# A whole model block on one core: first panel's low halves on VectorE, head 0 loaded under the gate, and a routing table built in one pass

## The reference

```
h = rmsnorm(x);  z = h @ w_in                       # q, k, v, gates, convolution: 4096 columns
q, k = rope(q), rope(k)                             # 12 heads of 64
o = three dilated causal windows, mixed by softmax of their log-sum-exp
conv = c_b * causal_conv3(c_c * c_h)
x = x + rmsnorm(concat(o * silu(g_attn), conv * silu(g_conv)) @ w_out)
... second block: gated mixer, cross attention to 256 memory rows, then
g = argmax over 4 groups;  the 2 best of that group's 8 experts;  gate = p(group) * softmax of the 2
tokens sorted by expert into blocks of 128 rows that each belong to one expert
y[block] = (silu(xb @ w1[e]) * (xb @ w3[e])) @ w2[e]
out = rmsnorm(x + sum over the 2 choices of gate * y)
```

## Time and profile before

| | us |
|---|---|
| median of 3 runs | 2814.45 (2813.74 to 2818.86) |
| profiled execution | 2812.59 |
| its span, first to last instruction | 2810.8 |
| TensorE busy | 2565.9 (91%) |
| VectorE busy | 1320.9 (47%) |
| ScalarE busy | 1184.0 (42%) |
| GpSimd busy | 633.9 (23%) |

### The profile page before, as it was taken

How to read it: one execution, slowest core, us unless ns; L and a number is a source line. 1 busy time by engine, 2 the same in 40 slices (tenths; PEclk the granted TensorE clock), 3 DMA queues, 4 the chain that set the end, 5 groups by cost and what they waited for, 6 DMA issues and landing times. The chain is left out here.

```text
span 2810.8 us, 30841 instructions
## 1 busy us (share of the span) xinstructions
PE 2565.9 (91%) x12104; PEld 2082.5 (74%) x12104; DVE 1320.9 (47%) x1716; ACT 1184.0 (42%) x1709; POOL 633.9 (23%) x520
## 2 busy tenths in 40 slices
PE   7999988879899999989998879898994999999992
PEld 6888866668687878868887668785784888888881
DVE  5530217764213212133434643105216888888885
ACT  4212137763241212123322432324323777777772
POOL 2312303323221213123211542345111111111100
PEclk9999999999999999999999989999996999999996
DMA  5433145523210131132225522332245899999985
GB/s 176 150 118 108 41 111 135 135 66 118 98 61 30 45 120 59 61 84 98 75 75 178 168 96 83 130 129 101 93 157 195 358 373 377 381 378 381 378 359 207
DMA packets 168690, 455.78 MB, mean 162 GB/s; under 512 B 17920, under 2 KB 85664, under 8 KB 155872
## 3 DMA queue, kind: packets, MB, share of 16 engines
q1 hardware_dynamic: 117856, 384.98, 38.0%
q10 hardware_dynamic: 37760, 41.17, 4.2%
q0 software_dynamic: 12928, 27.63, 2.8%
HBM read 389.23 MB, written 82.31 MB: 168 GB/s over the span
## 5 line engine op out<-in xcount | busy, mean ns | idle before, releaser
L2634 DVE TENSOR_TENSOR ex_w_lo<-ex_w,ex_w_hi 128x2048 fp32r<-128x2048 f32 x198 | 448.1, 2291 | 82.3 <-ACT ex_w_hi L2579 80.4
L2579 ACT ACTIVATE ex_w_hi<-ex_w 128x2048 fp32r<-128x2048 f32 x198 | 378.9, 1915 | 51.7 <-PEq L2180 26.4
L219 POOL TENSOR_TENSOR p_w_lo<-w_raw,p_w_hi 128x512 fp32r<-128x512 f32 (+1 forms) x154 | 203.1, 1350 | 644.4 <-ACT p_w_hi L239 620.0
L219 POOL TENSOR_TENSOR p_w_lo_rest<-w_raw,p_w_hi_rest 128x512 fp32r<-128x512 f32 x94 | 125.3, 1368 | 266.9 <-ACT p_w_hi_rest L239 266.9
L264 PE MATMUL o_ps<-o_w_hi,o_m_hi 128*128 128x512 f32 x384 | 154.4, 402 | 11.0 <-DVE split_cols L1133 11.0
L266 PE MATMUL o_ps<-o_w_hi,split_cols 128*128 128x512 f32 x384 | 152.6, 397 | 0.0
L265 PE MATMUL o_ps<-o_w_lo,o_m_hi 128*128 128x512 f32 x384 | 152.3, 397 | 0.0
L264 PE MATMUL p_ps<-p_w_hi,hT_hi 128*128 128x512 f32 (+1 forms) x320 | 120.9, 378 | 0.0
L266 PE MATMUL p_ps<-p_w_hi,hT_lo 128*128 128x512 f32 (+1 forms) x320 | 118.4, 370 | 0.0
L265 PE MATMUL p_ps<-p_w_lo,hT_hi 128*128 128x512 f32 (+1 forms) x320 | 118.1, 369 | 0.0
L2446 POOL DMA_INDIRECT ex_x<-xn_rows,slot_token x33 | 36.0, 1092 | 360.7 <-PE ex_px L2493 325.8
(11 more groups left out here) (435 smaller groups left out, 6460.1 us busy)
## 6 DMA issues: line engine op xcount, KB each, us to landing
ex_w<-w SPq DMA_DIRECT2D x99, 2048.0 KB, 13.9
w_raw<-w_in SPq DMA_DIRECT2D x42, 1024.0 KB, 5.1
x_rows<-o_x SPq DMA_DIRECT2D x24, 512.0 KB, 2.6
att_k<-k_columns SPq DMA_DIRECT2D x46, 256.0 KB, 7.4
w_raw<-w_out SPq DMA_DIRECT2D x8, 1024.0 KB, 9.5
qk_columns<-qk_y ACTq DMA_DIRECT2D x16, 512.0 KB, 2.6
o_x<-x_rows SPq DMA_DIRECT2D x16, 512.0 KB, 3.7
w_raw<-w_xkv SPq DMA_DIRECT2D x8, 1024.0 KB, 6.1
```

Of the source, the lines that this page charges most:

```text
L219: emit(self.lo(n)[:, 0:w], self.half(n // (KC // 2), w)[:, n % (KC // 2), :], self.hi(n)[:, 0:w].bitcast(F32), ALU.subtract).then_inc(self ...
L2579: nc.scalar.activation(w_hi[:, n % RING, :], raw_half(n), ACT.Copy).then_inc(hi_done, 1)
L2634: nc.vector.tensor_tensor(w_lo[:, n % RING, :], raw_half(n), w_hi[:, n % RING, :].bitcast(F32), ALU.subtract).then_inc(down_lo if m == "w2 ...
```

## The change

- **First panel.** ScalarE measures rows 0 and rows 1 before it rounds any weight, keeps rows 0's high half, rounds all eight chunks of the first panel, and then keeps rows 1's. VectorE, and no longer GpSimd, takes the low halves of these eight chunks, between the low halves of rows 0 and rows 1. GpSimd waits for them and goes on with later panels.
- **Head 0.** Attention's buffers for head 0's q and k, for the mask table and for v are made before the first stage. The first two share the place of the convolution's scratch `conv_z`, v's is the stage's own v buffer. At the end of its stream in the first stage, SP waits for the stores of q, k and v and for the convolution, then loads head 0, the mask table and v. Attention's SP starts with head 1; ScalarE and GpSimd issue no loads there, and ScalarE no longer waits at the end of the first stage.
- **Routing.** The clearing of semaphores before it goes. Three tables are set first. `first_of_max` drops an addition. Counts become one scan. Both choices' ranks are computed together (`both`, `wide`). The comparison for spare blocks moves behind the one-hot tables. `d1` and `d2` are fp32r; `d2` has two halves, token numbers and a mark for the second choice, so that 16 products with 96 columns give both tables. `d1` is made in four pieces, and TensorE starts on each. `slot_token` comes first, and GpSimd gathers the first two blocks inside routing, as soon as it is there.
- **Experts.** VectorE takes x's low half before the third weight half's.

```diff
+class HeadBuffers:
+    def __init__(self, c, stack):
+        with nc.sbuf_tensor("conv_z", [P, 4, S], F32) as self.conv_z:
+            pass
+        self.spare = stack.enter_context(nc.sbuf_tensor("att_first", [P, 3, S], F32R))
+        self.logc = stack.enter_context(nc.sbuf_tensor("logc", [P, S], F32))[:, :]
+        self.v_rows = stack.enter_context(nc.sbuf_tensor("att_v", [P, 2, 2 * BANK], F32R))
...
@@ project_first, SP @@
                 weights.load(sp, 2)
                 sp.wait_ge(c.const_rest, 16)
+                for b in range(2):
+                    sp.wait_ge(qk_out[b], 32 * n_qk // 2)
+                    sp.wait_ge(lo_out[b], 32 * n_qk // 2)
+                    sp.wait_ge(v_out[b], 16 * (n_v - n_qk) // 2)
+                sp.wait_ge(conv_done, CW // P)
+                for half in range(2):
+                    heads.load_qk(sp, 0, half, q_dram, k_dram)
+                sp.dma_start(heads.logc, c.const_dram("logc")).then_inc(heads.logc_in, 16)
+                heads.load_v(sp, 0, v_dram)
@@ project_first, GpSimd @@
-                weights.take_los(pool)
+                pool.wait_ge(weights.lo_done, KC)
+                weights.take_los(pool, (KC, weights.n_chunks))
@@ project_first, VectorE @@
-                for t in range(NT):
+                scale_rows(0)
+                scale_rows(1)
+                take_low_rows(0)
+                for n in range(KC):
+                    weights.take_lo(dve, nc.vector.tensor_tensor, n)
+                take_low_rows(1)
+                for t in range(2, NT):
                     scale_rows(t)
-                    if t >= 1:
+                    if t >= 3:
                         take_low_rows(t - 1)
@@ project_first, ScalarE @@
                 measure_rows(0)
-                take_high_weights(0, 2)
                 measure_rows(1)
                 take_high_rows(0)
-                take_high_weights(2, 8)
+                take_high_weights(0, KC)
+                take_high_rows(1)
...
-                for b in range(2):
-                    act.wait_ge(qk_out[b], 32 * n_qk // 2)
...
@@ attention @@
-                for h in range(NH):
+                for h in range(1, NH):
...
-                pool.dma_start(logc[:, :], c.const_dram("logc")).then_inc(logc_in, 16)
...
-                load_head(act, 0, 1)
@@ route, GpSimd @@
-                nc.gpsimd.memset(xg[:, :, :], 0.0)
+                nc.gpsimd.memset(xg[:, :, :], 0.0).then_inc(cleared, 1)
+                pool.wait_ge(cleared, 1)
+                pool.wait_ge(slots, 1)
+                for b in range(2):
+                    gather_rows(nc, xg, xn, slot_token, b, g_in[b])
@@ route, TensorE @@
-                pe.wait_ge(placed, 1)
-                for n in range(2 * NT):
-                    ins = pe.matmul(pt[:, 0:NBLK], d1[:, n, :], d2[:, n, :], start=(n == 0), stop=(n == 2 * NT - 1))
+                for i in range(2 * NT):
+                    k, t = 1 - i // NT, i % NT
+                    if i % 4 == 0:
+                        pe.wait_ge(placed, i // 4 + 1)
+                    ins = pe.matmul(pt[:, 0:2 * NBLK], d1[:, k * NT + t, :], d2[:, k, t, :, :].rearrange("p a b -> p (a b)"),
+                                    start=(i == 0), stop=(i == 2 * NT - 1))
@@ route, VectorE @@
+                V.memset(d2[:, 0, :, 1, :].bitcast(F32), 0.0)
+                step(V.memset(fresh[:, :, :], 1.0))
+                step(V.memset(fresh[:, :, 0:1], 0.0))
...
-                    step(V.tensor_scalar(idx[:, :], idx[:, :], 64.0, None, ALU.add))
...
-                step(V.memset(counts[:, 0, :], 0.0))
-                for t in range(NT):
-                    step(V.tensor_tensor(counts[:, t + 1, :], counts[:, t, :], pn[:, 0, t, :], ALU.add))
+                step(V.tensor_tensor_scan(counts[:, :, :].rearrange("p e t -> p (e t)"),
+                                          fresh[:, :, :].rearrange("p e t -> p (e t)"),
+                                          pn[:, 0, :, :].rearrange("p e t -> p (e t)"), 0.0, ALU.mult, ALU.add))
...
+                step(V.tensor_tensor(wide[:, :, :, :], both[:, :, :, :],
+                                     seen[:, :, :].rearrange("p e t -> p t e").unsqueeze(1).to_broadcast([P, 2, NT, NE]),
+                                     ALU.mult))
+                step(V.tensor_reduce(rank[:, :, :], wide[:, :, :, :], AX, ALU.add))
...
+                for i in range(4):
+                    k, t = 1 - i // 2, i % 2 * (NT // 2)
+                    V.tensor_tensor(d1[:, k * NT + t:k * NT + t + NT // 2, :],
+                                    c.const("iota").unsqueeze(1).to_broadcast([P, NT // 2, P]),
+                                    lo[:, k, t:t + NT // 2].unsqueeze(2).to_broadcast([P, NT // 2, P]), ALU.is_equal
+                                    ).then_inc(placed, 1)
...
@@ experts, GpSimd and VectorE @@
-                gather(0)
-                gather(1)
                 gather(2)
...
-                for n in range(3):
-                    take_lo(n)
+                take_lo(0)
+                take_lo(1)
                 keep_x(0)
+                take_lo(2)
@@ build @@
-            c.retire_semaphores(expert_weights.sems)
```

More of the change, by code:

```diff
@@ L690, in attention @@
         ps_o = s.enter_context(nc.psum_tensor("att_ps_o", [P, 2, BANK], F32))
-        logc_in = c.sem("logc_in")
-        qk_in, v_in = [c.sem(f"att_qk_in{b}") for b in range(2)], [c.sem(f"att_v_in{b}") for b in range(2)]
+        logc_in, qk_in, v_in = heads.logc_in, heads.qk_in, heads.v_in
         scored, maxed, expd = c.sem("att_scored"), c.sem("att_maxed"), c.sem("att_expd")
@@ new lines, in _ @@
+                step(V.tensor_tensor(wide[:, :, :, :].rearrange("p k t e -> p (k t) e"),
+                                     both[:, :, :, :].rearrange("p k t e -> p (k t) e"),
+                                     move[:, :].unsqueeze(1).to_broadcast([P, 2 * NT, NE]), ALU.mult))
+                step(V.tensor_reduce(over[:, :, :], wide[:, :, :, :], AX, ALU.add))
+                step(V.scalar_tensor_tensor(over[:, :, :], rank[:, :, :], float(P), over[:, :, :], ALU.is_ge, ALU.mult))
+                step(V.scalar_tensor_tensor(rank[:, :, :], idx12[:, :, :], float(P), rank[:, :, :], ALU.mult, ALU.add))
@@ new lines, in _ @@
+                step(V.tensor_tensor(dest_f[:, :, :], rank[:, :, :], over[:, :, :], ALU.add))
+                step(V.tensor_copy(lo_i[:, :, :], dest_f[:, :, :]))
+                step(V.tensor_scalar(lo_i[:, :, :], lo_i[:, :, :], P - 1, None, ALU.bitwise_and))
+                step(V.tensor_copy(lo[:, :, :], lo_i[:, :, :]))
+                step(V.tensor_tensor(hi[:, :, :], dest_f[:, :, :], lo[:, :, :], ALU.subtract))
+                for k in range(2):
+                    ins = V.tensor_tensor(d2[:, k, :, k, :], c.const("blk").unsqueeze(1).to_broadcast([P, NT, NBLK]),
+                                          hi[:, k, :].unsqueeze(2).to_broadcast([P, NT, NBLK]), ALU.is_equal)
@@ new lines, in _ @@
+                step(ins)
+                for k in range(2):
+                    V.scalar_tensor_tensor(d2[:, k, :, 0, :], c.const("tokid").unsqueeze(2).to_broadcast([P, NT, NBLK]),
+                                           1.0, d2[:, k, :, k, :].bitcast(F32), ALU.add, ALU.mult)
+                for i in range(4):
[4 more added lines that the diff above has]
+                                    ).then_inc(placed, 1)
@@ L2343, in load, with experts @@
             sp.dma_start(self.w2s[j][:, :], self.w2[at].rearrange("e p n -> (e p) n")).then_inc(self.w2_in[j], 16)
-def experts(c, weights, xn, y_rows, slot_token, slot_row, n_rest, xg, x3, tail):
+def experts(c, weights, xn, y_rows, slot_token, slot_row, n_rest, xg, g_in, x3, tail):
     nc = c.nc
@@ L2837, in build @@
             xg = late.enter_context(nc.sbuf_tensor("ex_x", [P, 2, D], F32))
-            route(c, expert_weights, logits, bias, gates, slot_token, slot_row, extra_expert, n_rest, xg)
+            g_in = [c.sem(f"ex_g_in{j}") for j in range(2)]
+            route(c, expert_weights, logits, bias, gates, slot_token, slot_row, extra_expert, n_rest, xg, xn, g_in)
             tail = combine_buffers(c, expert_weights)
-            experts(c, expert_weights, xn, y_rows, slot_token, slot_row, n_rest, xg, x3, tail)
+            experts(c, expert_weights, xn, y_rows, slot_token, slot_row, n_rest, xg, g_in, x3, tail)
             combine(c, tail, y_rows, gates, io["out"])
```

169 lines of the change are left out of this document (80 added, 89 removed).

## The result

The changed kernel takes 2794.56 us (median of 4 runs, 2791.41 to 2797.75) where the kernel before takes 2816.33 (4 runs, 2813.74 to 2818.86): a ratio of 0.9925, interval 0.9913 to 0.9938. A second measurement, of 5 runs against 9, gave 2793.01 and 2814.39, ratio 0.9926 (0.9912 to 0.9939). The profiled execution took 2791.41 us, span 2789.6.

The account below looks back on a forecast made before the run. TensorE was taken as the bound behind three places where it stood idle. Gains of 3.4 + 10.3 + 9.3 = 23.0 us from the profiled 2812.59 gave 2789.6, forecast as a 2791 median; range 2784 to 2801.

Parts of the forecast that it names:

- its three terms: Gains forecast at the first panel (3.4 us), head 0's loads (10.3) and routing (net 9.3).
- Opening, forecast 3.4: First panel: products start at 16.3 instead of 20.23, less 0.4 to 0.5 us waiting for rows 2.
- Rival 2: Opening: VectorE becomes the bound, its low halves delay rows 1 and 2; gain only 0.4, 2794 us; chance 0.10.
- My lower bound of 0.4: First panel: least gain, 0.4 us, if VectorE's low halves cost what GpSimd's did.
- Head 0, forecast 10.3: Attention's start: scores begin at about 391.1 instead of 402.01, then wait for head 1's keys until 401.0.
- Rival 3: Attention's start: head 0's loads effectively no earlier, or head 1's replace them; gain 0 to 4, 2797 to 2801; chance 0.10.
- rival 4: Attention runs at half clock, up to 10.8 us more a head, 2920 us in all; chance 0.04.
- Routing up to the gather, forecast 11.0: Routing, from end of scoring to first gather: shorter operation chain, one-pass table product and earlier gather win 11.0 us.
- the end of routing: Behind the first gather: barrier waits only for gathers' issue, ScalarE's rounding 2.95 us behind the gather; loss 1.7.
- rival 1: Routing's closing barrier waits for gathers to land, not be issued: 5 us more before ScalarE starts, 2796; chance 0.12.
- The second gather, though, went as chosen: End of routing: second gather takes 1.08 us, not the 2.96 traced before, as VectorE has stopped.
- That a start moved there moves the end: At all three edited places TensorE is the bound behind, so an earlier start there shortens the kernel.

Follow-up runs that it names:

- the run of the opening alone: Kernel before with only VectorE taking the first panel's low halves and ScalarE's new order: 2811.40 us in one run.
- the run of head 0 alone: Kernel before with only head 0's buffers and loads moved into the first block, head 1 loaded at attention's start: 2801.91 us in one run.
- The edit to `seen`: Changed kernel without routing's drain, `seen` kept token tile by token tile, and ScalarE measuring rows 2 before rows 1's high halves: 2787.62 us in one run.
- the run with eight more drains left out: Changed kernel with `seen` reordered and GpSimd's drain left out after routing, experts and eight more blocks: 2785.92 us, 0.9895 to the kernel before.

## Why the prediction was right, and where it was not

The time was right: 2791 forecast, medians of 2794.56 and 2793.01, inside 2784 to 2801. Two of its three terms were right as they were worked out, the third was right up to the gather and wrong behind it.

**Opening, forecast 3.4, measured 3.41.** Second turn 14.86 (14.7), first product 16.45 (16.3), wait for rows 2 0.45 (0.4 to 0.5). VectorE's halves took 0.62 each (2.49 for four). Rival 2, VectorE as the bound, is refuted: its last half ends at 20.32, and TensorE doesn't wait for it. What the term left out is the clock behind the first product. The stretch at 1.2 GHz was 1.3 us in the profiled run and 4.0 us in the run of the opening alone, so the same part gave 2.05 to 3.41 us at the stage's end. My lower bound of 0.4 doesn't follow from its own terms: 26.0 + 0.7 is 26.7, where the first group ended before (26.68), so it should have been 0.

**Head 0, forecast 10.3, measured 10.84, alone 10.45 to 10.9.** Head 1's first transfer goes out at 387.62 and TensorE waits for it until 397.04, 9.4 us later; I had taken 10.1 from head 3. Rival 3 is refuted by it. So is rival 4, slower by the half clock: 1.00 in 424 to 442, with TensorE busy 15.35 of 18.00 us among short gaps. The rule behind it in the Trainium skill (TensorE: Matmul & The Clock Gate, A second HAM failure mode: psum-queue depth-cycling) is not borne out by this stage. In other runs with the early head there is one stretch of 3.4 us at 0.50 at the end of the wait for head 1's keys (from 400.5 in the run of head 0 alone), and 1.00 from there to the scores of the last head.

**Routing up to the gather, forecast 11.0, measured 10.4.** The block started 0.26 us behind scoring where 0.5 was taken, the memsets cost 0.87 (0.75), the scan 0.69 (0.65), the table product 3.65 (3.5), from its end to the gather 1.50 (1.4). What missed most is the multiply by `seen`: I gave all four 512-wide steps 0.73, and this one, whose second input is read with the experts far apart, took 1.08. The edit to `seen` shows that the stride was the reason.

**The step that failed is the end of routing.** I put ScalarE's first expert rounding 2.95 us behind the start of the first gather, taking the barrier to wait until the gathers are issued; it came 6.58 behind it, and the loss behind the gather was 5.3 us instead of 1.7. With routing's drain left out it was 0.53, with the gathers behind the barrier it no longer depended on them: the barrier holds GpSimd's drain, and the drain, 6.01 us long, waits until the gathers have landed. That is rival 1, at 3.6 us instead of the 5 that I gave it, with a chance of 0.12. The argument against it, that nothing in the block waits on their semaphore, looked at the program's own waits only. Routing was worth 5.1 us at the experts' first product, not 9.3, and 2.6 at their last scatter. That a start moved there moves the end failed here in part, too: no new wait of TensorE took it back, but the clock.

The second gather, though, went as chosen: 1.01 us. With the gathers back behind the barrier it took 2.95 again, issued at 2120.26 while VectorE's subtract, begun at 2120.03, was running; the third gather took 2.37 under such a subtract in the changed kernel and 1.00 in the run without the drain, where it starts as the subtract ends. By the rule of the Trainium skill (SBUF — State Buffer, Who interferes with whom) it should be so, and these traces agree.

**Why the sum held all the same.** 3.41 + 10.84 + 5.13 = 19.4 us from the edited places, where 23.0 was forecast. The profiled execution was 21.2 us shorter and the medians 21.8 and 21.4 apart. In the profile the difference is 4.3 us won in unchanged stages, less the 2.5 lost in the experts. One of these stages ran at another granted clock: the scores at the end of scoring took 6.13 us for 32 against 6.88. In the medians I can't place the 2 us; the interval of the ratio, 17 to 25 us, holds 19.4 as well. So a term that was 4.2 us too large, and 2.5 us lost behind it, are in part hidden by luck.

## What to carry to other kernels

An asynchronous transfer that is issued ahead of a block's end isn't behind you: look at what the barrier itself waits for, and see whether the engine that issued it has to drain. In these runs a drain that was left out was paid at the next one, the closing stage's, where nothing waited for GpSimd. Where a part is worth a few microseconds, read it from its own stage, from a fixed point just ahead of it; the time of the whole kernel moves by as much with the clock of stages that nobody touched. And before moving a step of one engine forward, write down what stands ahead of its consumer on the next engine.

## What the runs showed of the hardware that I had not expected

GpSimd's drain at a block's end waits for its transfers to land (routing's ended 0.1 us behind the landing of the second gather), and behind landed ones it has a price that grows with the transfers issued since the drain before: 0.23 us behind 2, 2.84 behind 34, 5.29 behind 64, 5.46 behind 66. That is 0.08 us for each, gather or scatter, and the drains behind 4 and 16 ordinary transfers of GpSimd fit it (0.41 and 1.39 us). One row doesn't: in the run with eight more drains left out, 29 ordinary transfers came ahead of the drain at a clearing of semaphores, and it took 0.10 us. What takes the time is not shown.

The wait at the experts' end was 9.10 us instead of 9.71 in the two runs that left out only routing's drain. Their drain took 5.46, so the difference lies ahead of it: it began 3.40 us behind the last scatter's start instead of 4.18, as GpSimd went through the tests of its loop faster. Why it did so stays open.

A 512-wide multiply in fp32 with one input read in steps of 8 elements took 1.08 us instead of 0.69, a 256-wide addition that writes with such a stride 0.59 to 0.62 instead of 0.42.
